# Attention of a hybrid encoder layer: float32 products against split fp32r products with the projections placed between its steps

## What is computed

```python
x = x + 0.5 * swiglu_ffn(x, *ffn1)          # D_FF 2816
h = rms_norm(x, mix_g)
qa, ka, va, qb, kb, vb, fl = split(h @ w_in)   # 8+2+2 heads (A), 8+8+8 heads (B) of 64, 8 forget logits
qa, ka, qb, kb = rms_norm of each head; logf = log_sigmoid(fl + b_f)
# A: chunks of 64 queries over 192 keys (own chunk and two before), GQA 8:2
sa = qa @ ka.T / 8 + bias(rel);  w = exp(sa - m) / (sum + exp(sink - m));  o_a = w @ va
# B: 8 heads, causal over all keys, F = cumsum(logf)
sb = qb @ kb.T / 8 + F_q - F_k, masked;  o_b = softmax(sb) @ vb
x = x + (sigmoid(h Wg_a) * (o_a W_a) + sigmoid(h Wg_b) * (o_b W_b)) @ W_out
x = x + 0.5 * swiglu_ffn(x, *ffn2);  x = x + sigmoid(rms(x) W_pg) * (p W_pp)
```

## Time and profile before

| | us |
|---|---|
| median of three runs | 2968.4 |
| profiled execution, span | 2970.9 |
| TensorE busy | 2831.7 |
| VectorE busy | 1457.9 |
| ScalarE busy | 782.6 |
| GpSimd busy | 110.1 |
| mean granted TensorE clock | 0.947 |
| FFN 1 to the end of its norm | 0 to 839.6 |
| attention with its projections | 839.6 to 1603.7 |
| merge, FFN 2, embedding | 1603.7 to 2970.9 |

### The profile page before, as it was taken

One profiled execution on the slowest core, in us unless ns is written; L12 is line 12 of the kernel. 1 busy time (PEld: TensorE's weight loads), 2 busy tenths in 40 slices (PEclk: granted clock), 3 DMA queues, 4 the chain that ended last, 5 costly groups with the idle time before them and its releaser, 6 DMA issues.

```text
span 2970.9 us, 42305 instructions
## 1 busy us (share of the span) xinstructions
PE 2831.7 (95%) x15668; PEld 2588.3 (87%) x15668; DVE 1457.9 (49%) x2692; ACT 782.6 (26%) x1439; POOL 110.1 (4%) x164
## 2 busy tenths in 40 slices
PE   6999999999979989998998999998999999999989
PEld 6999999999976657676676888987999999999989
DVE  6444444444574555454543424337444444444654
ACT  4111111111243443534534111124111111111241
POOL 0000000000120000100100000003000000000120
PEclk9999999999996767999989999999999999999999
DMA  3111111111110001011012101110111111111112
GB/s 128 50 43 44 43 43 43 50 44 43 66 71 22 11 25 37 30 66 38 30 52 82 50 29 36 56 43 34 45 44 43 43 46 48 43 43 43 58 36 82
DMA packets 41567, 139.99 MB, mean 47 GB/s; under 512 B 5105, under 2 KB 10649, under 8 KB 40753
## 3 DMA queue, kind: packets, MB, share of 16 engines
q1 hardware_dynamic: 38256, 133.03, 13.2%
q10 hardware_dynamic: 3136, 4.47, 0.4%
HBM read 122.90 MB, written 16.15 MB: 47 GB/s over the span
## 4 chain that ended last, share of the span: by engine, by line
PE 89%; DVE 6%; issue 2%; ACT 2%; DMA 1%; ACTq 0%; SPq 0%; DVEq 0%
PE psum L396 71%; PE psum L559 5%; PE psum L524 5%; PE psum L658 4%; PE psum L541 3%; DVE h_lo L976 2%; DVE x L1035 1%; PE psum L485 1%; DVE root L1069 1%; DMA w_raw<-w_units 0%; DVE w_lo L362 0%; DVE sumsq L1155 0%; ACT probs_t L804 0%; DMA x<-x_t 0%; PE psum L454 0%
## 5 line engine op out<-in xcount | busy, mean ns | idle before, releaser
L396 PE MATMUL psum<-h_hi,w_hi 128*128 128x364 f32 (+1 forms) x3144 | 1061.3, 338 | 63.7 <-DVE h_lo L976 39.9
L396 PE MATMUL psum<-h_lo,w_hi 128*128 128x364 f32 (+1 forms) x3144 | 1046.1, 333 | 0.0
L396 PE MATMUL psum<-h_hi,w_lo 128*128 128x364 f32 (+1 forms) x3144 | 1045.1, 332 | 0.0
L396 PEld LDWEIGHTS psum<-h_hi,w_hi 128*128 128x128 f32 x3144 | 602.2, 192 | 75.6 <-issue 53.0
L396 PEld LDWEIGHTS psum<-h_lo,w_hi 128*128 128x128 f32 x3144 | 602.1, 191 | 5.1 <-issue 0.3
L396 PEld LDWEIGHTS psum<-h_hi,w_lo 128*128 128x128 f32 x3144 | 601.4, 191 | 0.0
L396 PE MATMUL psum<-hid_hi,w_hi 128*128 128x364 f32 x1296 | 428.4, 331 | 7.8 <-DVE x L1035 5.1
L396 PE MATMUL psum<-hid_lo,w_hi 128*128 128x364 f32 x1296 | 425.3, 328 | 0.0
L396 PE MATMUL psum<-hid_hi,w_lo 128*128 128x364 f32 x1296 | 424.9, 328 | 0.0
L1035 DVE SCALAR_TENSOR_TENSOR x<-psum,x 128x364 f32<-128x364 f32 (+1 forms) x624 | 317.0, 531 | 146.4 <-PE psum L396 145.4
L358 ACT ACTIVATE w_hi<-w_raw 128x1024 fp32r<-128x1024 f32 x185 | 194.3, 1050 | 513.0 <-PE psum L396 495.6
(11 more groups left out here) (118 smaller groups left out, 1976.9 us busy)
## 6 DMA issues: line engine op xcount, KB each, us to landing
w_raw<-w_units SPq DMA_DIRECT2D x193, 512.0 KB, 3.3
f_keys<-f_cumulative SPq DMA_DIRECT2D x4, 1600.0 KB, 7.2
x_saved<-x SPq DMA_DIRECT2D x8, 544.0 KB, 2.7
x<-x_saved SPq DMA_DIRECT2D x8, 544.0 KB, 7.6
y_out<-x SPq DMA_DIRECT2D x8, 544.0 KB, 4.1
x<-x_t ACTq DMA_DIRECT2D x2, 1456.0 KB, 9.6
kb_out<-k_t SPq DMA_DIRECT2D x4, 544.0 KB, 3.1
vb_out<-v_t SPq DMA_DIRECT2D x4, 544.0 KB, 3.0
```

The source lines that it names most:

```text
L396: mm = pe.matmul(out, w[:, slot, w_cols], m, start=first and n == 0, stop=last and n == 2)
```

## The change

All other stages keep their code. In the mixer:

- A **slot** is one block of 128 queries and both heads of a tile: 9 slots in 8 tiles, 72 in place of 144 steps. The sample's 64 queries are padded to 128.
- **Scores at full shape.** q and k are split into an fp32r part and a rest. The 128 rows of the loaded operand are q_hi (64) and q_lo (64); the moving one has k_hi twice. A second matmul adds q_hi against k_lo. In branch B the free 64 rows of the second one also hold a row of ones against F_hi and F_lo, so the forget term is in the product, and a third matmul of an identity with the triangle adds the mask. There is no F_q term (it cancels in the softmax). In branch A the sink is a 257th column of scores, with the bias.
- **Exponential, transposes, product.** In B the exponential reads PSUM. Probabilities are not scaled before they are turned. A **part** is up to four turned blocks: ScalarE rounds it (part_hi), VectorE subtracts (part_lo). For each block part_hi is loaded and [v_hi, v_lo] moves (128 columns), then part_lo is loaded and v_hi moves (64). VectorE adds the halves (`output`), GpSimd scales by the inverse sum (`normed`) into token rows, TensorE turns them back (`heads_out`), and they go to DRAM; at the end of the stage all of `o_t` is loaded from there.
- **Norms per head** are sums over each block by 2 moving columns (`head_stats`), a reciprocal of 18 columns, a spread by GpSimd and transposes (`spread`). Squares are GpSimd's.
- **Order.** 5 units (15 chunks) run ahead. The other 14 units, 1008 matmuls, are cut into pieces of 3 to 12 and stand at two places of a slot (`fill_count`, `mix_fill`): 16 per slot in the first tile and the first four slots of the second, 12 to 0 in the rest of A, 24 in B, none in the last slot of tile 6 and in tile 7. Norms, values, keys and queries of the next tiles have fixed slots (`side_steps`). Scores run one slot ahead, except at a tile's start. The code is written out, without loops.
- SyncE loads the merge's first weights before `o_t` and x.

```diff
+def fill_count(tile, idx, ph):
+    if tile < 2:
+        if tile == 0 or idx < 4 or (idx == 4 and ph == "p1"):
+            return 8
+        return 3 if idx > 4 else 0
+    if tile < PAIRS:
+        return 6 if idx < 4 else (3 if idx > 4 else 0)
+    if tile < 6 or (tile == 6 and idx < 8):
+        return 12
+    return 0
...
+            def scores(g):
...
+                if st.a:
+                    if g >= 2:
+                        pe.wait_ge(top_done, 2 * (g - 1))
+                elif SLOT[g - 1].a:
+                    pe.wait_ge(top_done, 2 * g)
+                else:
+                    pe.wait_ge(exp_done, 2 * g)
...
+                        pe.matmul(out, q1[:, c0:c0 + P], k1[:, keys], start=True, stop=False)
+                        mm = pe.matmul(out, q2[:, c0:c0 + P], k2[:, keys], start=False, stop=not diagonal)
+                        if diagonal:
+                            mm = pe.matmul(psum_flat[:, at + c + n - P:at + c + n], ident_r[:], tri_r[:], start=False,
+                                           stop=True)
...
+            def product(k):
+                g, i = PARTS[k]
+                st = SLOT[g]
+                if i == 0:
+                    if g:
+                        pe.wait_ge(o_copied, g)
...
+                pe.wait_ge(part_lo_done, k + 1)
+                for n, (h, j) in enumerate(st.parts[i]):
+                    cols = slice(n * P, (n + 1) * P)
+                    b, end = st.vals[j], j == len(st.vals) - 1
+                    pe.matmul(psum[:, 7, h * P:(h + 1) * P], part_hi[:, k % 2, cols], val[:, b, h, :],
+                              start=j == 0, stop=False)
+                    mm = pe.matmul(psum[:, 7, h * P:h * P + HD], part_lo[:, k % 2, cols], val[:, b, h, 0:HD],
+                                   start=False, stop=end)
+                mm.then_inc(pv_done, 1)
...
+            for g in range(N_SLOTS):
+                more = g + 1 < N_SLOTS
+                if more and early(g + 1):
+                    scores(g + 1)
+                turn(g, 0)
+                mix_fill((g, "p1"))
+                side((g, "p1"))
+                if g:
+                    product(last_part(g - 1))
+                mix_fill((g, "p2"))
+                side((g, "p2"))
+                for i in range(1, len(SLOT[g].parts)):
+                    turn(g, i)
+                    product(PART_NO[g, i - 1])
+                side((g, "end"))
+                if more and not early(g + 1):
+                    scores(g + 1)
...
+            for g in range(N_SLOTS):
+                more = g + 1 < N_SLOTS
+                ahead = more and early(g + 1)
+                k0, parts = PART_NO[g, 0], len(SLOT[g].parts)
+                turned_hi(k0)
+                if ahead:
+                    exponent(g + 1, 0)
+                place_act((g, "p1"))
+                place_act((g, "p2"))
+                if parts > 1:
+                    turned_hi(k0 + 1)
+                if ahead:
+                    exponent(g + 1, 1)
+                for i in range(2, parts):
+                    turned_hi(k0 + i)
+                place_act((g, "end"))
```

More of the change, by code:

```diff
@@ L33 @@
 BANKS = 6
-STAT_K = 5
 U_FFN = FF_GROUPS * 6
@@ new lines, with last_part @@
+SLOT = [Slot(g) for g in range(N_SLOTS)]
+PARTS = [(g, i) for g in range(N_SLOTS) for i in range(len(SLOT[g].parts))]
+PART_NO = {key: k for k, key in enumerate(PARTS)}
+def last_part(g):
+    return PART_NO[g, len(SLOT[g].parts) - 1]
+def fill_count(tile, idx, ph):
[8 more added lines that the diff above has]
+    return 0
@@ new lines @@
+DENSE_STEPS = {5: [("sq", ("k", 0))], 7: [("stat", ("k", 0))], 8: [("spread", ("k", 0)), ("keys", 0)],
+               10: [("values", 0)], 11: [("sq", ("q", 0))], 12: [("stat", ("q", 0))], 13: [("spread", ("q", 0))],
+               14: [("queries", 0)]}
+PLACES = [("dense", i) for i in range(DENSE)] + [(g, ph) for g in range(N_SLOTS) for ph in ("p1", "p2", "end")]
+FILL, STEPS_AT = {}, {}
+done = 0
+for place in PLACES:
+    if place[0] == "dense":
+        n, STEPS_AT[place] = 3 * KD, DENSE_STEPS.get(place[1], [])
+    else:
+        tile, idx = divmod(place[0], SLOTS)
+        n = fill_count(tile, idx, place[1]) if place[1] != "end" else 0
+        STEPS_AT[place] = side_steps(tile, idx, place[1])
+    FILL[place] = range(done, done + n)
+    done += n
@@ new lines, with early @@
+for i in range(DENSE):
+    small_results(STEPS_AT["dense", i])
+for g in range(N_SLOTS):
+    T_KEYS.append(("part", g, 0))
+    small_results(STEPS_AT[g, "p1"])
+    small_results(STEPS_AT[g, "p2"])
+    T_KEYS.extend(("part", g, i) for i in range(1, len(SLOT[g].parts)))
+    small_results(STEPS_AT[g, "end"])
+small_results([("out", TILES - 1, 1), ("out", TILES - 1, 2)])
+T_NO = {key: t for t, key in enumerate(T_KEYS)}
+assert len(T_NO) == len(T_KEYS)
+GROUPS3 = [(0, 4), (4, 4), (8, 1)]
+def early(g):
+    return g % SLOTS != 0
@@ new lines, in _ @@
+            exponent(0, 0)
+            exponent(0, 1)
+            for g in range(N_SLOTS):
+                more = g + 1 < N_SLOTS
[13 more added lines that the diff above has]
+                place_act((g, "end"))
+                if more and not ahead:
+                    exponent(g + 1, 0)
+                    exponent(g + 1, 1)
@@ new lines, in _ @@
+            dve.wait_ge(psum_free, MIX["e"] + DENSE)
+            dve.memset(psum[:, 1:5, 2 * P:2 * P + 1], 0.0).then_inc(sink_cols, 1)
+            tops(0)
+            for g in range(N_SLOTS):
+                more = g + 1 < N_SLOTS
+                k0, parts = PART_NO[g, 0], len(SLOT[g].parts)
+                if more and early(g + 1):
+                    tops(g + 1)
+                turned_lo(k0)
+                inverse(g)
+                place_dve((g, "p1"))
+                if g:
+                    output(g - 1)
+                place_dve((g, "p2"))
+                for i in range(1, parts):
+                    turned_lo(k0 + i)
+                place_dve((g, "end"))
+                if more and not early(g + 1):
+                    tops(g + 1)
@@ L1440, in _ @@
[L1440 to L1450 removed]
+            value_cache(0)
```

1375 lines of the change are left out of this document (754 added, 621 removed).

## The result

Four executions of the kernel before had a median of 2966.6 us, four of the changed kernel 2855.3 us (2847.6 to 2860.5): a ratio of 0.9623, 95% interval 0.9598 to 0.9647. The change wins 111 us. The forecast was 148 us (2968.4 to 2820), so sign and place were right and a quarter of the size was missing. The profiled execution took 2847.6 us, its span is 2845.8.

A forecast was written before the change was run, and what follows sets the result against it. TensorE was taken as the bound, with 264 of the attention stage's 764 us lower clock and waiting. Work 498 plus 123 exposed makes 621; 2970.9 - 143 - 6 = 2822 profiled, so 2820 us as median, range 2745 to 2910.

The forecast's parts named there:

- The sum of work: TensorE in the attention stage: all its instructions at the full clock take 498 us, equal to the work before.
- the 166 ns rival: Short fp32r matmuls in attention cost 166 ns each, not 112: +66 us of work, less 20, total 2866; chance 0.20.
- The term that failed: the clock: Lower clock in the attention stage: 15 us for the last tile and long waits, 4 us for the first unit.
- The clock does not come back: Rival: clock stays near 0.65 in half of the attention, so 160 us of work grow by 80: 2900; chance 0.10.
- The exposed waits: TensorE's waits in the attention stage that stay uncovered, 104 us in all without the clock's 19.
- Tile starts: 8 slots not scored ahead expose result, minimum, two exponentials and handovers, 2.3 us each: 18 us.
- Splitting: Splitting new keys and queries in slot 7 delays copies products wait for: 5 us in four tiles, 1.5 in three, 25 us.
- Last tile: Without projections, four wide slots expose 2.5 us each and each first product waits 0.5 us: 15 us.
- Later parts in branch B: Way round of 1.7 us against 1.33 us of TensorE work, in 56 parts without projections between: 20 us.
- Norms: Table loads of 1.28 us for 13 norms stand ahead of exponentials on ScalarE, some 2 us each: 26 us.
- The slower rival: Fixed order stalls on the way round in all 72 slots, 3 us each, and 56 parts: 311 us, 3010; chance 0.07.
- Merge: Weights load ahead of the reload of x, so the second unit no longer waits: 6 us won; worst, 3 lost.

The follow-up runs named there:

- Run 1: Changed kernel with each tile's projections of slots 0 to 7 put in one block in slot 1: 2958.7 us, 0.9942 of the kernel before.
- run 4: Changed kernel without the product of the probabilities' low halves with the values (464 instructions): 2810.8 us, 0.9456 of the kernel before.
- run 3: Changed kernel splitting only 64 columns of new keys and queries from the second tile on: 2819.5 us, 0.9475 of the kernel before.
- run 2: Changed kernel with the square root of the 13 query and key norms made a plain copy: 2848.5 us, 0.9571 of the kernel before.
- run 10: Changed kernel loading the merge's second and third unit weights behind attention outputs and x again: 2872.7 us, 0.9666 of the kernel before.

## Why the prediction was right, and what it missed

*The sum of work: right.* 498 forecast, 485 found. Some 10 of the 13 us are the 28 ns behind the last turn of each of 128 parts, where I had charged 109. The other way, the first score matmul of a 512-column piece is followed 282 ns later and the second 230, where I had 216 for each. The price that decided it, 112 ns for a short fp32r matmul, taken from the row with 128 loaded and 8 moving columns, is 110 in the gaps and 108 by leaving 464 out. Neither bound nor the 166 ns rival came near. With 128 loaded columns and up to 128 moving ones the price hardly moves in this trace: 111 ns with 2 (the sums of squares), 109 with 128 (the turns), 110 as the mean of a pair with 128 and 64.

*The gain is lower clock and waiting: right.* By one way of grouping the gaps, work is 491 us before and 480 after, lower clock 108 and 50, waiting 165 and 118; the low level lasts 269 us before and 149 after. Run 1 shows that the rest of the change without the place of the projections brings 8 us of stage.

*The term that failed: the clock.* "I take 15 us for the last tile and the long waits, and 4 us for the first unit", 19 together, measured 53 and 62 us in two executions. I had held that branch A would be above 0.95, with projections in 60 of 72 slots. Branch A as a whole, then one tile of it, show this:

```profile
918.00:1107.00 189.00, 167.73 (x1094) 160.39 (x1094) 109.47 (x318) 92.81 (x221) 34.16 (x55) 0.88 0.15 45
...
998.00:1041.00 43.00, 38.25 (x243) 36.19 (x242) 23.93 (x76) 21.07 (x54) 8.46 (x15) 0.84 0.11 32
...
1083.00:1125.00 42.00, 30.56 (x167) 27.59 (x166) 22.82 (x43) 19.82 (x37) 4.34 (x7) 0.76 0.25 66
```

The last row, with the 5.4 us wait in it, is at 0.76. I priced waits only by their length; the low slices that come with them cost half as much again (53 us beside 111). The term came out 34 us higher, work 13 lower and waits 7 higher: together the 28 us by which the first profiled stage is longer than 621. The last two are of the size of the doubt in the grouping, the first is well over it. "The clock does not come back" was a rival at 2900 with 0.10; what came is 34 of its 80 us.

The total alone would have misled: 2855 lies 35 us from my 2820 and 11 from the 2866 of the 166 ns rival. Only the spacing of the matmuls and run 4 tell that the missing time is clock and not the price of an instruction. Of the signs that I had named as right, the stage near 620 (649 and 658) and the clock over 0.95 in branch A (0.88) did not come.

*The exposed waits: near in sum (104 against 111), uneven in parts*, so that the sum is partly luck: what I had charged too much for later parts and norms is near what no term had. I sorted the gaps of the first trace by place:
- Tile starts: forecast 18, found 28. I had missed the ninth transpose of values, which waits 1.1 us for its bank, and the 1.6 us of scores behind it, in four tiles.
- Splitting: forecast 25, found 29, and with the clock that follows 28 to 41 by run 3.
- Last tile: forecast 15, found 13, with 10 more of lower clock.
- Later parts in branch B: forecast 20, found some 5. A part goes round in 1.7 us, but two are under way at a time, so TensorE goes from one part to the next in the 1.25 us of its own work (1234.97 to 1236.22) and now and then waits 0.35 us (ahead of 1236.98); I had charged the latency.
- Norms: forecast 26, found 3 to 12 (run 2), and 7 for their spread transposes. The loads mostly lie under 12 projections; only three in branch A touch a wait.
- The rest, some 30 us, are gaps of under half a microsecond that no term had.

*The slower rival* needed 3.5 us in every slot; the first turns and products wait that long in only a few slots. *VectorE and ScalarE* are busy 345 and 278 us in the stage, where I had 365 and 315; neither is near 649. *Merge*: 6 us forecast, 8 found (5 to 9 over the runs that leave it as it is, but for 1 in run 4), and no wait on o_t; run 10 shows the wait that would be there.

## What to carry to other kernels

Where an in-order engine runs chains with a way round over two others, try independent work between the steps first: here, with the new products in place, that was 107 of 115 us, and all the rest 8. Whether it would have done as much between the old products is not tested. When pricing what stays exposed, charge a wait for its length and for the lower clock behind it (half as much again here), and charge a pipelined part its period and not its latency (1.25 and 1.7 us here). Then look for the long passes that stand in a row ahead of one short one, and for what they feed (here a copy by DMA of 5 us): moving them without moving that copy gave one wait for another. Moving them to another engine is not free either: VectorE's own pass of 64x1600 beside GpSimd's took 3.7 to 4.0 us in place of 1.8.

## What was not expected of the hardware

- The same program with the same waits (111 and 112 us) spent 149 us of the stage at a granted clock of 0.50 in one execution and 174 in another, 9 us of time apart. Single profiles of this stage can't settle less than that in time; the waits by themselves repeated to 1 us.
- Pairs of fp32r matmuls with 128 loaded columns and 128 and 64 moving ones start 142 and 79 ns apart, not at even spacing; only their mean is 110, near the 111 of the sums with 2 moving columns.
- A copy of 64x1152 from one half of the partitions to the other by DMA lands 4.5 to 5.6 us after its issue (the changed kernel's eight), and GpSimd subtracts 64x1600 in 3.6 us, in part beside VectorE's pass, where VectorE by itself takes 1.8.
- While GpSimd does that subtraction, VectorE's of the same shape takes 3.7 to 4.0 us; a copy of 64x1152 on GpSimd takes 1.1 us, and 2.2 beside a subtraction on VectorE.
- 18 us of matmuls added to the last tile changed the total by nothing that the 9 us of doubt let through: they went into waits (4 to 5 us fewer) and into clock that had been lost (8 to 17).
